# Modulation weights in 128-column pieces between weight slabs, a new order of the attention steps, low halves on VectorE alone

## What is computed

```python
# first block, per layer
u = h @ w_in
proj = einsum("bsnc,ncd->bsnd", [y_ssm, y_fox, y_moba, y_dsa], w_branch)
merged = sum(sigmoid(h @ w_gate + b_gate) * proj);  mix = merged @ w_out
x = x + rms_norm(mix);  x = x + rms_norm(swiglu(rms_norm(x)))
# second block, per layer, for the tokens (c) and the context (c_ctx)
sh1, sc1, g1, sh2, sc2, g2 = split(silu(c) @ w_mod + b_mod, 6)    # w_mod: 1024 x 6144
p = modulate(rms_norm(x), sh1, sc1) @ w_in
o = diff_attention(q, k, v)              # two softmaxes per head, subtracted
x = x + g1 * (merge(gmlp(p), o, conv(p)) @ w_out)
x = x + g2 * ((silu(dwconv(h2 @ w_gate)) * (h2 @ w_val)) @ w_down)
```

## Time and profile before

| | |
|---|---|
| median of three runs | 2511.81 us (2507.24 to 2511.85) |
| the profiled execution | 2500.43 us |
| its span, first to last instruction | 2498.8 us |
| TensorE / VectorE / ScalarE / GpSimd busy | 2247.9 / 1425.2 / 1044.5 / 303.8 us |
| mean granted TensorE clock | 0.940 |

### The profile page before, as it was taken

The page is one execution under the profiler, slowest core; times in us unless marked ns, Lnnn a source line. Parts: engine busy times, 40 slices in busy tenths (PEclk is TensorE's granted clock), DMA queues, the critical chain, the costliest instruction groups (busy, mean ns, idle before and its releaser), DMA issues. The chain is left out here.

```text
span 2498.8 us, 29164 instructions
## 1 busy us (share of the span) xinstructions
PE 2247.9 (90%) x11116; PEld 1796.6 (72%) x11116; DVE 1425.2 (57%) x2187; ACT 1044.5 (42%) x1664; POOL 303.8 (12%) x310
## 2 busy tenths in 40 slices
PE   8999898898999998979997877889989898887999
PEld 6777676787777776768876664667767787656997
DVE  5665574454465647545445886554444325966774
ACT  4545554443444455534443434322222223543443
POOL 0017120000000532210000540000000000600000
PEclk9999999999999999989998988889999998987999
DMA  7644335565555433466564213423333435333554
GB/s 227 185 124 127 105 115 160 181 177 183 191 175 157 141 102 95 138 201 180 160 205 159 63 51 93 135 93 110 101 101 110 135 101 168 94 119 117 162 183 161
DMA packets 184121, 349.15 MB, mean 140 GB/s; under 512 B 11824, under 2 KB 23216, under 8 KB 183984
## 3 DMA queue, kind: packets, MB, share of 16 engines
q1 hardware_dynamic: 183984, 347.29, 44.4%
HBM read 346.19 MB, written 1.05 MB: 139 GB/s over the span
## 5 line engine op out<-in xcount | busy, mean ns | idle before, releaser
L816 DVE TENSOR_TENSOR wlo<-wraw,whi 128x1024 fp32r<-128x1024 f32 (+1 forms) x538 | 646.2, 1207 | 682.0 <-ACT whi L1009 678.7
L1009 ACT ACTIVATE whi<-wraw 128x1024 fp32r<-128x1024 f32 (+1 forms) x552 | 562.7, 1027 | 648.0 <-PE psum L1770 546.3
L1770 PE MATMUL psum<-whi,act_h 128*128 128x512 f32 (+2 forms) x1424 | 578.4, 406 | 31.8 <-DVE p L1320 22.1
L1770 PE MATMUL psum<-wlo,act_h 128*128 128x512 f32 (+2 forms) x1424 | 564.7, 397 | 0.0
L1770 PE MATMUL psum<-whi,act_l 128*128 128x512 f32 (+2 forms) x1424 | 563.8, 396 | 0.0
L1770 PEld LDWEIGHTS psum<-whi,act_h 128*128 128x128 f32 x1424 | 277.1, 195 | 105.6 <-DVE p L1320 24.7
L1770 PEld LDWEIGHTS psum<-whi,act_l 128*128 128x128 f32 x1424 | 275.7, 194 | 62.2
L1770 PEld LDWEIGHTS psum<-wlo,act_h 128*128 128x128 f32 x1424 | 276.6, 194 | 56.5
L1770 PE MATMUL psum<-act_h,whi 128*128 128x512 f32 (+1 forms) x704 | 244.0, 347 | 23.7 <-DVE wlo L816 19.8
L1770 PE MATMUL psum<-act_l,whi 128*128 128x512 f32 (+1 forms) x704 | 242.2, 344 | 0.0
L1770 PE MATMUL psum<-act_h,wlo 128*128 128x512 f32 (+1 forms) x704 | 242.2, 344 | 0.0
(11 more groups left out here) (270 smaller groups left out, 2693.4 us busy)
## 6 DMA issues: line engine op xcount, KB each, us to landing
wraw<-in_w_in SPq DMA_DIRECT2D x136, 512.0 KB, 3.7
wraw<-in_w_gate SPq DMA_DIRECT2D x104, 512.0 KB, 3.7
wraw<-in_w_mod SPq DMA_DIRECT2D x96, 512.0 KB, 3.7
wraw<-in_w_ffn_in SPq DMA_DIRECT2D x80, 512.0 KB, 3.7
wraw<-in_w_ffn_out SPq DMA_DIRECT2D x44, 512.0 KB, 4.2
wraw<-in_w_down SPq DMA_DIRECT2D x44, 512.0 KB, 4.3
wraw<-in_w_val SPq DMA_DIRECT2D x40, 512.0 KB, 4.6
wraw<-in_w_branch SPq DMA_DIRECT2D x32, 512.0 KB, 3.9
```

Of the source, the lines that this page charges most:

```text
L816: eng.tensor_tensor(wlo[:, i, 0:st.n, 0:st.w], wraw[:, st.s % RING_W, 0:st.n, 0:st.w], whi[:, i, 0:st.n, 0:st.w].bitcast(F32), ALU.subtrac ...
L1009: nc.scalar.activation(whi[:, d % RING_S, 0:st.n, 0:st.w], wraw[:, s % RING_W, 0:st.n, 0:st.w], ACT.Copy).then_inc(sem("slab_rounded"), 1)
L1770: return nc.tensor.matmul(out, lhsT, rhs, start=start, stop=stop)
```

## The change

- A chunk of modulation becomes four pieces of 128 columns by all 1024 rows, each one slot of the ring, from a weight array laid out anew so that a partition's 4 KB lie together. A piece is used in one step (`mod_ride`: 8 products of 128 columns); its reader (`mod_reader`) is one step two slabs later. 96 pieces: 64 of columns, all in the first block, one behind the first slab of a column group; 16 of gates in the attentions of the second block, 8 per layer; 16 in its feed-forward stages, one behind every fifth slab, in bank 7, which leaves seven banks to the products. No chunk stands at a seam any more.
- The exponential of both attentions becomes a step of its own (`attn_e`, `att2_e`). Order in the first block: s(i), v(i-3), t(i-2), e(i). In the second: s(i), v(i-3), t(i-2), e(i), m(i-1).
- No low half is made on GpSimd. `p` is evicted by ScalarE alone.
- `pad_common` and `pad_one` are put in and `rstd4` is moved, so that `hid_h`, `act_h`, `y_h`, `act2_h` and `hid2_h` all begin 384 bytes past a multiple of 512. `whi` and `wlo` stay.
- `cond` (the silu of the condition) moves from before `w_out` to slab 10 of the first `w_in`.

```diff
@@ gemm
+            if pl.mod_every:
+                pl.mod_since += 1
+                if pl.mod_queue and pl.mod_since % pl.mod_every == 0:
+                    st.after = mod_ride(pl, pl.mod_bank)
+                elif pl.mod_since % pl.mod_every == pl.mod_gap:
+                    st.after = mod_reader(pl, pl.mod_bank)
+            elif (pl.mod_queue or pl.mod_last) and tiles == 2 and st.s >= 3 * RING_W:
+                at, slabs_in = k // SLAB_K, -(-nk // SLAB_K)
+                if pl.mod_queue and at % 4 == 0 and at + 3 < slabs_in:
+                    st.after = mod_ride(pl, pl.next_bank())
+                elif at % 4 == 2:
+                    st.after = mod_reader(pl, pl.next_bank())
...
+def mod_ride(pl, bank):
+    l, c = pl.mod_queue.pop(0)
+    n = len(pl.mod_reads) + len(pl.mod_last)
+    st = Step(kind="slab", s=len(pl.slabs), weight="w_mod_2", layer=l, c=c, evac="mod", mc=n, banks=[pl.bank(bank)],
+              first=True, last=True, war=pl.mod_reads[n - 2] if n >= 2 else [])
...
@@ plan_first
-                for kind, h in (("attn_s", i), ("attn_v", i - 3), ("attn_t", i - 2)):
+                for kind, h in (("attn_s", i), ("attn_v", i - 3), ("attn_t", i - 2), ("attn_e", i)):
...
-        for st in pl.slabs[first:-len(g)]:
-            st.pool = st.s % 3 == 0
...
-        mods = mod_slabs(pl, 0, filler.pop(0))
         ms = [split("scr", 256 * g, [("merged", pl.now("merged"))], "ym", 2 * g) for g in range(4)]
-        pl.steps += mods + ms + mod_reader(pl, mods, pl.misc)
+        pl.steps += ms
...
-        pl.steps += mods + waiting + mod_reader(pl, mods, pl.misc)
+        pl.steps += waiting
...
@@ plan_second
-            for kind, u in (("att2_m", i - 1), ("att2_t", i - 2), ("att2_s", i), ("att2_v", i - 2)):
+            for kind, u in (("att2_s", i), ("att2_v", i - 3), ("att2_t", i - 2), ("att2_e", i), ("att2_m", i - 1)):
...
+        pl.mod_queue = [(l, c) for c in MOD_GATES[0]]
+        stream = [agate] + mod_ride(pl, pl.gemm_turn()) + mod_ride(pl, pl.gemm_turn())
+        for i in range(2, KD + 2):
+            stream += mod_reader(pl, pl.gemm_turn())
+            if i < KD:
+                stream += mod_ride(pl, pl.gemm_turn())
...
+        pl.mod_queue, pl.mod_every, pl.mod_since = [(l, c) for c in MOD_GATES[1]], 5, 0
-        pl.turns = tuple(range(8))
+        pl.turns = tuple(range(7))
...
+        def at_offset(name, stack):
+            n = (OPERAND_AT - nc.sbuf_base) % OPERAND_STEP
+            if n:
+                sb(name, [P, n // 4], F32, stack)
+        at_offset("pad_common", ctx)
...
+        at_offset("pad_one", one)
...
-        rstd4 = sb("rstd4", [P, 4], F32, two)
...
+        rstd4 = sb("rstd4", [P, 4], F32, two)
...
@@ sync: the ring
                 if st.s >= RING_W:
                     was = slabs[st.s - RING_W]
                     need(sp, [was.used if was.evac == "mod" else was.split])
+                if st.evac == "mod":
+                    sp.dma_start(wraw[:, st.s % RING_W, :, :].rearrange("p k n -> p (k n)"), A["w_mod_pieces"][st.layer, st.c]
+                                 ).then_inc(sem(f"slab_landed{st.s % RING_W}"), 16)
+                    continue
@@ scalar
                     if st.evac == "p":
-                        for t in range(0, st.tiles, 2):
+                        for t in range(st.tiles):
...
@@ vector
-                    if st.evac == "p":
-                        for t in range(1, st.tiles, 2):
-                            filled(dve, st.banks[t])
-                            dve.tensor_copy(p[:, t, st.col:st.col + st.w], psum[:, st.banks[t][0], 0:st.w]
-                                            ).then_inc(free(st.banks[t]), 1)
...
@@ tensor
+                    for k in range(KD):
+                        r = 32 * (k % 4)
+                        ins = dot(psum[r:r + 32, bk[0], 0:P], condm[:, k, :], w[:, k * P:(k + 1) * P], k < 4, k >= 4)
+                    ins.then_inc(full(bk), 1)
```

More of the change, by code:

```diff
@@ L49 @@
 RING_W, RING_S, AHEAD = 4, 4, 3
+OPERAND_AT, OPERAND_STEP = 384, 512
 SLAB_K = 2
@@ L174, in gemm @@
             pl.slabs.append(st)
-            if evac != "mod":
-                st.d = len(pl.dense)
-                pl.dense.append(st)
+            st.d = len(pl.dense)
+            pl.dense.append(st)
             steps.append(st)
-    return steps
[L182 to L192, removed]
@@ new lines, in gemm @@
+    return steps
+MOD_COLS = list(range(0, 2 * KD)) + list(range(3 * KD, 5 * KD))
+MOD_GATES = (list(range(2 * KD, 3 * KD)), list(range(5 * KD, 6 * KD)))
+def mod_ride(pl, bank):
[3 more added lines that the diff above has]
+              first=True, last=True, war=pl.mod_reads[n - 2] if n >= 2 else [])
+    b, use = st.banks[0]
+    st.used = (f"psum_full{b}", use + 1)
+    pl.slabs.append(st)
+    pl.mod_last.append(st)
+    return [st]
@@ new lines, in mod_reader @@
+def mod_reader(pl, bank):
+    if not pl.mod_last:
+        return []
+    st = pl.mod_last.pop(0)
+    l, c, part = st.layer, st.c, st.c // KD
+    bk = pl.bank(bank)
+    pl.mod_reads.append([(f"psum_full{bk[0]}", bk[1] + 1)])
+    if part in (2, 5):
+        return [Step(kind="mod_gate", l=l, c=c, mc=st.mc, gate=part // 3, j=c % KD, waits=drained(*st.banks), banks=[bk])]
+    steps = [Step(kind="mod_cols", l=l, c=c, mc=st.mc, waits=drained(*st.banks), banks=[bk])]
+    if part in (1, 4) and c % KD == KD - 1:
+        steps.append(Step(kind="mod_gain", l=l, i=part // 3, waits=drained(bk)))
@@ L209, in mod_reader @@
     return steps
 def plan_first(pl):
-    filler = list(MOD_COLS)
+    pl.mod_queue = [(i, c) for i in range(DEPTH) for c in MOD_COLS]
     for l in range(DEPTH):
@@ L268, in plan_first @@
                (36, Step(kind="decay_turn", **decay)), (37, cb)]
+        if l == 0:
+            ssm.append((10, Step(kind="cond")))
         ybanks = [pl.bank(6), pl.bank(7)]
@@ L393, in plan_first @@
             hidden += waiting
-        mods = mod_slabs(pl, 0, filler.pop(0))
-        pl.steps += mods + waiting + mod_reader(pl, mods, pl.misc)
+        pl.steps += waiting
         out = gemm(pl, "w_ffn_out", l, "hid", 2, KF, 0, D, "mix", ready=split_ready(hidden))
         pl.steps += out
[L398 to L404, removed]
+        postnorm(2 * l + 1, out)
 def plan_second(pl):
-    filler = [(0, MOD_COLS[-1])] + [(1, c) for c in MOD_COLS]
+    assert not pl.mod_queue and not pl.mod_last
+    pl.mod_bank, pl.mod_gap, pl.turns = 7, 2, (0, 1, 2, 3)
     for l in range(DEPTH):
@@ L566, in plan_second @@
             pl.tick("hid_lo", w // P)
-            if late:
-                pl.steps += mod_reader(pl, late, pl.misc)
-            late = fill() if c in (0, 1, 2, 3) else None
-            pl.steps += late or []
-        late = fill()
-        pl.steps += late
-        if late:
-            pl.steps += mod_reader(pl, late, pl.misc)
+        assert not pl.mod_queue and not pl.mod_last
+        pl.mod_every = 0
         pl.turns = (0, 1, 2, 3)
@@ L591, in build @@
         plan_second(pl)
+    pl.steps = [one for st in pl.steps for one in [st] + st.after]
     slabs, dense = pl.slabs, pl.dense
```

130 lines of the change are left out of this document (50 added, 80 removed).

## The result

| | before | after |
|---|---|---|
| median | 2511.83 us | 2444.55 us (2439.43 to 2448.31, four runs) |
| profiled execution / its span | 2500.43 / 2498.8 us | 2442.91 / 2441.3 us |
| mean granted TensorE clock | 0.940 | 0.951 |

The ratio to the kernel before is 0.9734, with a 95% interval from 0.9712 to 0.9757. That is 67 us less, where 137 were forecast. The direction was right, the size was not: the time lies outside the range, and half of the gain is missing.

What follows compares the result with a forecast made beforehand. TensorE was taken as the bound, 2247.9 of 2498.8 us busy. Terms 38 + 54 + 26 + 12 + 7 = 137 us off the profiled 2500.4 gave 2363, as a median 2374 us; range 2330 to 2435.

Steps and rivals of the forecast that it cites:

- modulation: Chunks at seams replaced by pieces in dense stretches: 138 us gained, 84 us paid, net 54 us less.
- low halves: GpSimd's low halves, no longer made there: predicted to change nothing.
- Queues: Slab four places behind a piece arrives late; TensorE has 8.4 us of slabs ready: covered, 2 us to spare.
- Rival 4: The ring starves: slabs later than 8.4 us make rides small seams; sign decided from 1.7 us a ride; chance 0.05.
- What else the pieces cost: Pieces and readers in dense stretches: 84 us; pieces in the second block's attentions taken as free.
- Rides: A piece's matmuls within a dense stretch: 0.8 us each; a column reader 0.2, a gate reader 0.45.
- Seams: Places between stages and column groups where modulation chunks and readers stood: removing them gains 138 us.
- Operands: Stationary tiles moved to 384 bytes past a multiple of 512: 6.6 ns less per 512-column matmul, 38 us, bounds 0 to 41.
- rival 1: The operand address is not the cause of the faster matmuls; 38 us don't come, 2412 us; chance 0.15.
- Attention, first block: ScalarE copies turned probabilities before waiting for the next maxima: 12 us less, bounds 0 and 21.
- Attention, second block: Next maxima before the mix cover VectorE's wait for the exponential; some 3.3 us a round; 26 us less, bounds 10 and 40.
- `p`: ScalarE alone evicts `p`: 7 us of 22.4 us of waits gained, bounds 0 and 22; the q and k norm wait grows.

Runs made afterwards that it cites:

- ring5: The changed kernel with five places in the ring instead of four, pieces still in the ring: ratio 0.9594 to the kernel before, 2406.3 us.
- before_addr: The kernel before with only the new places of the operands: ratio 0.9901 to the kernel before, 2480.9 us.
- p_split: The changed kernel with the odd row blocks of `p` evicted by VectorE again: ratio 0.9756 to the kernel before.
- before_ring5: The kernel before with five places in the ring instead of four, its chunks unchanged: ratio 0.9855 to the kernel before, 2472.8 us.

## Why the prediction was wrong

The parts measured one by one add up: -2 (modulation) + 17 (operands) + 21 and 25 (attentions) + 6 (`p`) + 2 (low halves) = 69 us, and the change gave 67. Each part is known to some 12 us, so that they meet so closely is in part luck. Against them stand the terms of the forecast, 54, 38, 26, 12, 7 and 0.

- **Queues, "covered, with 2 us to spare": the step that failed, with 35 us.** It asked whether the late slab is there when TensorE needs it. The delay of the load was taken rightly (5 us; issued at 2255.52, ScalarE begins on it at 2260.97). At most rides the slab is in time; the two waits of 4.5 us for `wlo` where it is not don't explain the 35, since `ring5` keeps them. But ScalarE works through its list in order and stood before loads for 220 us more than before, VectorE behind it, and what was queued there, evictions and with them banks, was late. The forecast named just this as what would make it wrong, and gave it neither a price nor a chance. Rival 4 had the right place and the wrong size: at 35 us for 96 pieces it is a fifth of the 1.7 us a ride from which it would decide the sign.
- **What else the pieces cost.** 84 us were forecast and 145 measured; the 35 leave 26 that no experiment takes apart. By the traces the pieces in the second block's attentions, taken as free, cost 19 (the chunks there had cost 30, not 7, so this was no loss against before). And with a place of their own for the pieces TensorE still has 14 us more of waits and 15 more of slow steps than without pieces; some 16 of slow steps are in the forecast's 0.8 a ride. What makes these waits stays open.
- **Rides.** 0.77 us and 0.23 for a column reader by their own rows, against 0.8 and 0.2: rightly priced. What was left out is the dense stream behind each interruption: some ten steps at 224 to 240 ns until it is back at 227, 5 us in all. The trace before had this in it, hidden by a stream that never settled (229 and 238 ns in turns). A rule of the Trainium skill was weighed here (TensorEngine Tiling (Array Packing), "Key Properties", a change of mode drains TensorE). The trace shows 0.31 us into the ride and 0.34 out of it, instead of 0.23 each: 0.2 us a ride, less than the 0.39 allowed for it. A column reader, two matmuls of 2 columns without a change of mode, has 0.23 into it and 0.31 out of it. So most of what is lost behind a ride any interruption costs, and the rule's drain can be no more than the rest, some 0.1 us.
- **Seams.** As the price of the chunks the term held, 116 found for 131. With the chunk gone, the stages round `w_out` (the norm behind it included) are shorter by 13.5 and 13.1 us against 16 each, those up to `w_ffn_out` by 9.8 and 8.4 against 11, the column groups with the next norm by 61.6 against 60.3. It failed at one norm, the one before the feed-forward stage, where 5.3 were taken and the chunk was free (-2.1). But the seams were priced without the pieces. At `w_ffn_out` of the first layer the stretch from the last product of `w_ffn_in` to the first of `w_ffn_out` went from 11.3 only to 8.4 us, since now rides and late slabs put the last of `hid` off: it is 4.5 with the fifth place and 3.2 without pieces. In the other layer, where the stage has few rides, it went from 11.0 to 2.5.
- **Operands.** The mechanism was right, rival 1 fell with two experiments. The size was not: 38 taken, 30 of steps found before and 25 after. Where the operands began at a multiple of 512, in most of the first block, the step was about 232.5 ns and not 233.3, and each interruption costs part of the gain again. The turned roles, for which 3 us were held back, gained as much as the others (233.4 to 227.4 ns). Of those 30, 25 reach the end by the ratio and 18 by the two traces: in `before_addr` TensorE's waits are 5.5 us longer (242.3 against 236.8) and the rest went into slow steps. The rule of the Trainium skill set against it (SBUF — State Buffer, "SBUF: two separate sides") says nothing of addresses, and the measurements decide: they matter to TensorE's step.
- **Attention, first block.** 25 (19 by the traces) against 12. Its bound of 21 counted the waits alone; slow steps behind the waits make 6 of the 19.
- **Attention, second block.** 21 (8 by the traces) against 26. The pace of 3.2 us a unit is as forecast. The waits turned: `aT` went down by 16 us, `e` L1476 came up by 6.
- **`p`.** No wait for L1320, a longer one for L1436, as forecast; but all of it went there, 22.4 us off and 21.8 on. The 6 us that `p_split` measures against 7 forecast can't be told from nothing.

The better kernel that the study leads to is the changed one with a fifth place in the ring or a place of their own for the pieces: 2406 us, 4% below the kernel before.

## What to carry to other kernels

When a buffer of a ring is held longer, don't only ask whether the consumer at the end still gets its data in time. Ask which in-order engines will stand before the late load, for how long, and what is queued behind them there. The view of their waits for loads shows that it happens (101 to 321 us on ScalarE here), but not what it is worth: `ring5` takes 180 us of these waits away and gains 35, `before_ring5` takes 24 away and gains 36. And before counting a stall as a gain, find in the trace what else would end at the same place: a chunk that stands in a wait is free.

## What the runs showed of the hardware

- TensorE's step for 512 fp32r columns with a weight load each depends on where the operand tiles begin against the weight tiles. With the weights 128 bytes past a multiple of 512, it is 226.7 ns with the operands at 128 or 384 (at 384 for instance in `w_down`), about 232.5 at 0 or 256, and 233.3 at 352. It is so with the operands stationary and the weights moving, and (352 against 384) the other way round. Why, no run shows. Steps of 256 columns go the other way, by some 1.4 ns (118.4 before, 119.8 after).
- After an interruption of a dense stream by other shapes, the step behind is 0.31 us (reader) to 0.34 us (ride) instead of 0.23, and some ten more steps swing between 224 and 240 ns before they settle at 227. With the operands at the poorer places they never settled (229 and 238 ns in turns, and 230 to 235).
